# First nine input blocks all laid out with tokens on the partitions, and seven of them turned by VectorE

## What the reference computes

```python
u = rms_norm(h, norm_mix[l])
z = u @ w_in[l]
(aq, ak, av, bxin, bgate, cq, ck, cv, cf, dq, dk, dv, gz) = jnp.split(z, split_points, axis=-1)
ya = diff_attention(aq, ak, av, lam, slopes_a)                 # q, k: features x tokens
yb = rg_lru_branch(bxin, bgate, conv_w, conv_b, wa, ba, ...)   # scan along the tokens
yc = forgetting_attention(cq, ck, cv, logf)
yd = sliding_window_sink_attention(dq, dk, dv, sinks, slopes_d)
mixed = sum(gates[:, :, n] * (branches[n] @ w_branch[l, n]) for n in range(4))
```

## Time and profile before

| | |
|---|---|
| time, median of 3 runs (lowest, highest) | 2922.37 us (2922.26, 2922.62) |
| the profiled execution's own time | 2922.03 us |
| its span | 2920.2 us |
| TensorE busy | 2898.1 us, 99% |
| VectorE busy | 1906.7 us, 65% |
| ScalarE busy | 1363.7 us, 47% |
| granted TensorE clock, mean | 1.00 |

### The profile page before, as it was taken

One profiled execution on the slowest core, in us unless ns is written; L12 is line 12 of the kernel. 1 busy time (PEld: TensorE's weight loads), 2 busy tenths in 40 slices (PEclk: granted clock), 3 DMA queues, 4 the chain that ended last, 5 costly groups with the idle time before them and its releaser, 6 DMA issues.

```text
span 2920.2 us, 33076 instructions
## 1 busy us (share of the span) xinstructions
PE 2898.1 (99%) x13622; PEld 2420.9 (83%) x13622; DVE 1906.7 (65%) x2448; ACT 1363.7 (47%) x1755; POOL 61.9 (2%) x108
## 2 busy tenths in 40 slices
PE   8999999999999999999999999999999999999999
PEld 8998788888887888888888888888888888888887
DVE  5666675669877674577785544555897667457664
ACT  5545544444554443444446555444444444344443
POOL 1000000000011000000001000000000000000000
PEclk9999999999999999999999999999999999999999
DMA  7455555555566555555555445555555555555554
GB/s 267 158 185 183 178 184 180 199 202 189 204 245 221 200 193 196 189 200 188 190 200 195 160 172 184 171 178 194 192 199 195 194 190 199 188 197 191 189 200 159
DMA packets 84103, 561.76 MB, mean 192 GB/s; under 512 B 10067, under 2 KB 10211, under 8 KB 19056
## 3 DMA queue, kind: packets, MB, share of 16 engines
q1 hardware_dynamic: 77760, 544.80, 54.4%
q0 software_dynamic: 3456, 10.01, 1.2%
q10 hardware_dynamic: 2736, 4.83, 0.6%
HBM read 557.50 MB, written 3.68 MB: 192 GB/s over the span
## 4 chain that ended last, share of the span: by engine, by line
PE 98%; DVE 1%; ACT 0%; DMA 0%; issue 0%; DVEq 0%; ACTq 0%
PE acc L620 95%; PE misc L620 2%; PE misc L624 1%; DVE w_lo L1410 1%; DMA xT<-in_xT 0%; ACT w_hi L986 0%; DMA lam_vec<-in_lam_vectors 0%; ACT prob L965 0%; DVE lru_work L1662 0%; ACT u_hi L968 0%; DVE turned L1410 0%; DVE prob L1416 0%; ACT L965 0%; ACT av L968 0%; DVE y_lru_lo L1410 0%
## 5 line engine op out<-in xcount | busy, mean ns | idle before, releaser
L1410 DVE TENSOR_TENSOR w_lo<-raw,w_hi 128x1024 fp32r<-128x1024 f32 x1032 | 1256.5, 1220 | 837.4 <-ACT w_hi L986 830.9
L986 ACT ACTIVATE w_hi<-raw 128x1024 fp32r<-128x1024 f32 x1032 | 1087.4, 1056 | 1240.2 <-PE acc L620 1239.2
L620 PE MATMUL acc<-w_hi,v_hi 128*128 128x512 f32 x1408 | 548.1, 389 | 0.0
L620 PE MATMUL acc<-w_hi,v_lo 128*128 128x512 f32 x1408 | 547.8, 389 | 0.0
L620 PE MATMUL acc<-w_lo,v_hi 128*128 128x512 f32 x1408 | 547.7, 389 | 0.0
L620 PE MATMUL acc<-w_hi,u_hi 128*128 128x512 f32 (+1 forms) x1248 | 493.2, 395 | 0.0
L620 PE MATMUL acc<-w_hi,u_lo 128*128 128x512 f32 (+1 forms) x1248 | 483.3, 387 | 0.0
L620 PE MATMUL acc<-w_lo,u_hi 128*128 128x512 f32 (+1 forms) x1248 | 482.6, 387 | 0.0
L620 PEld LDWEIGHTS acc<-w_hi,v_hi 128*128 128x128 f32 x1408 | 264.3, 188 | 57.4 <-issue 2.6
L620 PEld LDWEIGHTS acc<-w_hi,v_lo 128*128 128x128 f32 x1408 | 264.3, 188 | 54.8
L620 PEld LDWEIGHTS acc<-w_lo,v_hi 128*128 128x128 f32 x1408 | 264.3, 188 | 54.7
(11 more groups left out here) (310 smaller groups left out, 2956.7 us busy)
## 6 DMA issues: line engine op xcount, KB each, us to landing
raw<-in_w_gates SPq DMA_DIRECT2D x112, 1024.0 KB, 4.9
raw<-in_w_ffn_gate SPq DMA_DIRECT2D x88, 1024.0 KB, 4.8
raw<-in_w_ffn_up SPq DMA_DIRECT2D x88, 1024.0 KB, 4.8
raw<-in_w_ffn_down SPq DMA_DIRECT2D x88, 1024.0 KB, 4.8
raw<-in_w_in SPq DMA_DIRECT2D x67, 1024.0 KB, 4.8
raw<-in_w_out SPq DMA_DIRECT2D x32, 1024.0 KB, 4.8
raw<-in_w_branch SPq DMA_DIRECT2D x24, 1024.0 KB, 4.8
raw<-in_w_mem SPq DMA_DIRECT2D x8, 1024.0 KB, 4.9
```

The source lines that it names most:

```text
L620: return e.matmul(o, w, x, start=start, stop=stop, skip_group_check=True)
L986: e.activation(m.w_hi[:, n % PART_SLOTS, 0:HALF_KT * cols], m.raw[:, c % RAW_SLOTS, o * cols:(o + HALF_KT) * cols], ACT.Copy).then_inc(s[" ...
L1410: return e.tensor_tensor(o, a, b, op)
```

## The change

All nine blocks are computed with tokens on the partitions. Their inverse roots are then a column, and ScalarE applies them when it evacuates the accumulator. For `keep4` and `keep8` it writes to the final place, as before. The other seven go to a staging buffer `keep_tok`, and a new mover `keep_turn` on VectorE turns them in 16 transposes of 32 x 256 elements, four in each of the first four steps of the next block. One staging buffer serves all seven. The constant factors of the queries are put into two more columns (`r_q64`, `r_q128`). The row of inverse roots with its diagonal matrices, two products and copy is gone. Those who read the seven results now wait on `keep_turned`.

The order of the tasks is the same; `rows` has two steps fewer.

```diff
-    plan = [full(f"keep{b}", "w_in", b, "u", fm=0 if b == 4 else 4) for b in range(5)]
+    plan = [full(f"keep{b}", "w_in", b, "u") for b in range(5)]
...
+KEEP_TURNED = (0, 1, 2, 3, 5, 6, 7)
...
         evacuate("keep", plan[f"keep{b}"], b)
+        if b in KEEP_TURNED:
+            mover(f"keep_turn:{b}", plan[f"keep{b}"], b)
...
# TensorE, stream: the products of one row tile
-                for f in range(b.fm):
-                    o = v[:, f // 2, (f % 2) * SEQ:(f % 2 + 1) * SEQ]
-                    mm = matmul(o, tile(whi, f), lhi, first and f % 2 == 0, last)
-                    mm = matmul(o, tile(whi, f), llo, False, last)
-                    mm = matmul(o, tile(wlo, f), lhi, False, last)
...
+                for t in range(2):
+                    o = v[:, t, 0:b.cols]
+                    mm = matmul(o, tile(lhi, t), whi, first, last)
+                    mm = matmul(o, tile(lhi, t), wlo, False, last)
+                    mm = matmul(o, tile(llo, t), whi, False, last)
...
# TensorE, rows
-        matmul(bank[:, 0:P], m.ones[:, 0:P], m.diag_r[:, 0, :], True)
-        matmul(bank[:, P:2 * P], m.ones[:, 0:P], m.diag_r[:, 1, :], False).then_inc(s["rows_summed"], 1)
...
# ScalarE, evacuate
+        if kind == "keep":
+            n = more[0]
+            to, scale = m.keep[n], {2: m.r_q64, 5: m.r_q64, 6: m.r_q128}.get(n, m.r_mix)
             e.wait_ge(s["half_read"], b.done)
             e.wait_ge(s["row_root"], 1)
+            if n in KEEP_TURNED:
+                to = m.keep_tok
+                if n:
+                    e.wait_ge(s["keep_turned"], KEEP_TURNED.index(n))
...
+            scaled(to[:, 0, :], v[:, 0, :], scale[:, 0:1])
+            scaled(to[:, 1, :], v[:, 1, :], scale[:, 1:2]).then_inc(freed, 1)
...
# ScalarE, rows
-        scaled(m.r_rows[:, :], bank[:, 0:SEQ], 1.0).then_inc(s["rows_copied"], 1)
...
# VectorE, evacuate
-        if kind == "keep" and b.fm:
-            ...
-            stt(to[:, 0:2, :], v[:, 0, :].rearrange("p (a b) -> p a b", a=2), scale, rows, ALU.mult, ALU.mult)
-            stt(to[:, 2:4, :], v[:, 1, :].rearrange("p (a b) -> p a b", a=2), scale, rows, ALU.mult,
-                ALU.mult).then_inc(freed, 1)
...
# VectorE, rows
-        for t in range(2):
-            i = ts(m.diag_r[:, t, :], m.ident[:, :], m.r_mix[:, t:t + 1], ALU.mult)
+        ts(m.r_q64, m.r_mix, 64 ** -0.5, ALU.mult)
+        ts(m.r_q128, m.r_mix, 128 ** -0.5, ALU.mult).then_inc(s["q_scales"], 1)
+
+    def keep_turn(block, b):
+        e.wait_ge(s[f"acc_freed{block.slot}"], block.after)
+        yield from turn_squares(m.keep_tok[:, :, :], m.keep[b], 4, "keep_turned")
...
+    def turn_squares(tokens, turned, steps, done):
         squares = tokens.rearrange("p t (m n b) -> p t m n b", m=4, n=4)
         to = turned[:, :, :].rearrange("p m (t i b) -> p t m i b", t=2, i=4)
         for n in range(16):
             i, f = divmod(n, 4)
             mm = e.transpose(to[32 * f:32 * f + 32, :, :, i, :], squares[32 * i:32 * i + 32, :, :, f, :])
             if n == 15:
+                mm.then_inc(s[done], 1)
+            if (n + 1) % (16 // steps) == 0:
                 yield
```

More of the change, by code:

```diff
@@ L35, with __init__ @@
 class Block:
-    def __init__(self, label, name, b, k0, kn, cols, left, fm=0, frees=1):
+    def __init__(self, label, name, b, k0, kn, cols, left, frees=1):
         self.label, self.name, self.b, self.k0, self.kn, self.cols = label, name, b, k0, kn, cols
-        self.left, self.fm, self.frees = left, fm, frees
+        self.left, self.frees = left, frees
 def stream_plan():
     full = lambda label, name, b, left, **kw: Block(label, name, b, 0, KT, BW, left, **kw)
-    plan = [full(f"keep{b}", "w_in", b, "u", fm=0 if b == 4 else 4) for b in range(5)]
+    plan = [full(f"keep{b}", "w_in", b, "u") for b in range(5)]
     plan += [Block("keep_misc", "w_in_misc", 0, 0, KT, P + 4 + P, "u")]
-    plan += [full(f"keep{b}", "w_in", b, "u", fm=0 if b == 8 else 4) for b in range(5, 9)]
+    plan += [full(f"keep{b}", "w_in", b, "u") for b in range(5, 9)]
     for n, y in enumerate(("y_lru", "y_diff", "y_win", "y_fox")):
@@ L365, in __init__ @@
         self.q_sums, self.k_sums = spot("q_sums", r, 0, [4, SEQ]), spot("k_sums", r, 4, [4, SEQ])
-        self.diag_r, self.r_rows = spot("diag_r", q, 0, [2, P]), spot("r_rows", q, 1, [SEQ])
+        self.keep_tok = spot("keep_tok", q, 0, [2, BW])
         self.gate_w, self.decay, self.drive = (spot("lru_gate_w", q, 4, [8, P]), spot("decay", q, 8, [4, SEQ]),
@@ L622, in transposes @@
     def transposes(o, tiles, done):
+        need(("ident_landed", 16))
         for i, a in enumerate(tiles):
@@ L676, in rows, with turned @@
     def rows():
[L677 to L680, removed]
-        matmul(bank[:, 0:P], m.ones[:, 0:P], m.diag_r[:, 0, :], True)
-        matmul(bank[:, P:2 * P], m.ones[:, 0:P], m.diag_r[:, 1, :], False).then_inc(s["rows_summed"], 1)
-        bank_free[i] = ("rows_copied", 1)
+        yield 7
+    def keep_turn(block, b):
+        yield 4
+    def turned(b):
+        return ("keep_turned", KEEP_TURNED.index(b) + 1)
     def lru():
@@ L724, in diff @@
             banks = [task_bank(), task_bank()]
-            need(freed(plan["keep2"]))
-            need(freed(plan["keep3"]))
+            need(turned(2))
+            need(turned(3))
             paired_scores([bank for _, bank in banks], m.aqT[:, h, :], m.akT[:, h, :], "diff_pe")
@@ L760, in win @@
             need(("win_dve", WIN_DVE("dk")))
-            need(freed(plan["keep5"]))
+            need(turned(5))
             paired_scores([bank for _, bank in banks], m.dqT[:, j, :], m.dkT, "win_pe")
@@ L792, in fox @@
             need(("consts_landed", 16 * 11))
-            need(freed(plan["keep6"]))
-            need(freed(plan["keep7"]))
+            need(turned(6))
+            need(turned(7))
             need(("fox_dve", FOX_DVE("terms")))
@@ L949, in dil @@
             yield
-    work = {"x_move": x_move, "rows": rows, "lru": lru, "diff": diff, "win": win, "fox": fox, "gate_tanh": gate_tanh,
+    work = {"x_move": x_move, "rows": rows, "keep_turn": keep_turn, "lru": lru, "diff": diff, "win": win, "fox": fox, "gate_tanh": gate_tanh,
             "mixed_move": mixed_move, "row_squares": row_squares, "resid_move": resid_move, "ffn_rows": ffn_rows,
@@ L992, in bias_in @@
         if q == 0:
-            e.wait_ge(s[f"acc_freed{plan['keep7'].slot}"], plan["keep7"].after)
+            e.wait_ge(s["keep_turned"], len(KEEP_TURNED))
         elif q == 1:
@@ L1015, in evacuate @@
         freed = s[f"acc_freed{b.slot}"]
-        if kind == "keep" and not b.fm:
+        if kind == "keep":
+            n = more[0]
+            to, scale = m.keep[n], {2: m.r_q64, 5: m.r_q64, 6: m.r_q128}.get(n, m.r_mix)
             e.wait_ge(s["half_read"], b.done)
             e.wait_ge(s["row_root"], 1)
-            scaled(m.keep[more[0]][:, 0, :], v[:, 0, :], m.r_mix[:, 0:1])
-            scaled(m.keep[more[0]][:, 1, :], v[:, 1, :], m.r_mix[:, 1:2]).then_inc(freed, 1)
+            if n in KEEP_TURNED:
+                to = m.keep_tok
+                if n:
+                    e.wait_ge(s["keep_turned"], KEEP_TURNED.index(n))
+            if n == 2:
+                e.wait_ge(s["q_scales"], 1)
+            scaled(to[:, 0, :], v[:, 0, :], scale[:, 0:1])
+            scaled(to[:, 1, :], v[:, 1, :], scale[:, 1:2]).then_inc(freed, 1)
         elif kind == "keep_misc":
@@ L1110, in rows, with keep_turn @@
                            "x_squares", 2 * j + t + 1)
-        yield 3
-        bank = task_bank()
-        e.wait_ge(s["rows_summed"], 1)
-        scaled(m.r_rows[:, :], bank[:, 0:SEQ], 1.0).then_inc(s["rows_copied"], 1)
+        yield 2
+    def keep_turn(block, b):
+        yield 4
     def lru():
@@ L1437, in evacuate @@
         freed = s[f"acc_freed{b.slot}"]
-        if kind == "keep" and b.fm:
[L1439 to L1444, removed]
-            stt(to[:, 0:2, :], v[:, 0, :].rearrange("p (a b) -> p a b", a=2), scale, rows, ALU.mult, ALU.mult)
-            stt(to[:, 2:4, :], v[:, 1, :].rearrange("p (a b) -> p a b", a=2), scale, rows, ALU.mult,
-                ALU.mult).then_inc(freed, 1)
-        elif kind == "biased_gate":
+        if kind == "biased_gate":
             q = more[0]
@@ L1511, in moved @@
             if n == 15:
-                mm.then_inc(s["moved_turned"], 1)
-            if (n + 1) % per_step == 0:
+                mm.then_inc(s[done], 1)
+            if (n + 1) % (16 // steps) == 0:
                 yield
+    def moved(left, j, tokens, turned, gain=None):
+        yield from turn_squares(tokens, turned, turn_steps(j, left), "moved_turned")
         turn["moved"] += 1
@@ L1608, in lru @@
         yield
-        e.wait_ge(s[f"acc_freed{plan['keep0'].slot}"], plan["keep0"].after)
+        e.wait_ge(s["keep_turned"], KEEP_TURNED.index(0) + 1)
         for f in range(4):
@@ L1644, in lru @@
         yield
-        e.wait_ge(s[f"acc_freed{plan['keep1'].slot}"], plan["keep1"].after)
```

(1 more changed line is left out.)

11 lines of the change are left out of this document (3 added, 8 removed).

## The result

| | before | after |
|---|---|---|
| time, median of 13 runs | 2922.68 us | 2928.54 us |
| lowest to highest | 2922.15 to 2924.26 | 2926.90 to 2930.13 |
| profiled execution, its span | 2922.03, 2920.2 | 2928.97, 2927.2 |
| TensorE matmuls | 13622 | 12946 |
| VectorE busy | 1906.7 us | 1946.0 us |

The ratio is 1.0019 with a 95% interval of 1.0011 to 1.0027: slower by 5.9 us between the medians, with 2931 forecast. The two profiled executions are 6.9 us apart, their spans 7.0.

What follows compares the result with a forecast made beforehand. TensorE, busy 99% of the span, was taken as the bound. Terms -8.6 - 0.45 + 0.4 + 7.3 + 7.6 + 2.4 = +8.65 us, added to the median 2922.4, gave about 2931 us; range 2924.5 to 2935.5.

Steps and rivals of the forecast that it cites:

- Matmuls of 512 columns: TensorE in the nine blocks: each block 1.25 us shorter, 1.1 in `keep0`; sum -8.6 us.
- Evacuations on ScalarE: Seven blocks' evacuations move from VectorE to ScalarE; this and waiting for the single `keep_tok` cost nothing.
- The wait at the gate product: TensorE waits for conv33, late because VectorE's steps hold transposes: +7.3 us.
- The wait of 0.4 us in `keep2`: TensorE waits for the last `w_lo` of `keep2`, behind three steps of 3.05 us and small columns: +0.4 us.
- The waits in `diff`: TensorE's waits from the first `prob` through `keep6`, `keep7` and `keep8`: sum +7.6 us.
- First `prob`: Its chain does not hang on TensorE's spacing, so what nine shorter halves give goes into the wait: +1.4 us.
- The clock: TensorE's clock falls after the wait of 7.3 us at the gate product: +2.4 us, bounds 0 and 2.4.
- B: Rival: the waits come but without the slow clock, 2928.6 us; chance 0.25.
- A: The forecast itself: 2931 us; chance 0.47.
- C: Rival: only the gate product's wait is real, `diff` has more room; 2922.4 us, with the clock 2925; chance 0.15.
- D: Rival: VectorE's time is hidden and the matmul spacing comes through; 2913 us, faster; chance 0.05.
- E: Rival: more waits, the tail of `lru` beside `keep_misc` also comes late; +3 us, 2934; chance 0.08.

Runs made afterwards that it cites:

- copies_only: Kernel after with one copy of 128x256 in place of four transposes in each of the four steps, so results are wrong; 2913.24 us.
- spread: Kernel after with two transposes in each of eight steps instead of four in each of four; 2924.79 us.
- two_spread: spread with two staging buffers instead of one; 2920.82 us.
- tasks_first_spread: Kernel after with two transposes in each of eight steps, and task pieces before mover pieces while a block is turned; 2926.70 us.
- two_tf_spread: tasks_first_spread with two staging buffers instead of one; 2917.40 us.
- double_turn: Kernel after with each of the 16 transposes done twice, the second into a buffer nobody reads; 2961.14 us (one run).
- tasks_first: Kernel after with each engine doing a step's task piece before its mover piece while a block is turned; 2919.59 us.
- filler: Kernel after with 26 matmuls of 512 columns on TensorE ahead of the first gate product, their result overwritten; 2926.05 us.

## Why the prediction was right, and where its sizes were off

**Matmuls of 512 columns: right.** 21.76 us a block, forecast 21.79. In copies_only, where none of the new waits is left, the span is 9.7 us shorter, forecast 9.05; 2.6 of the 9.7 lie in `keep0`, where 1.55 were forecast and the profiles scatter. The rule of the Trainium skill ("TensorE: Matmul & The Clock Gate", section "Wait — 56ns, not 53.3ns?"), by which the spacing would have given 1.6 us, does not agree with any of these traces.

**Evacuations on ScalarE: right in the kernel after, but only because the turning ended in time.** I had written that waiting for the single buffer costs nothing since the block before is turned in the first half of this one. With eight steps it cost 4 us (spread against two_spread) and 9 us (tasks_first_spread against two_tf_spread).

**The wait at the gate product: right in mechanism and size.** VectorE went on 7.1 us after the start of `keep2` (7.3 forecast), had no pause, and ended conv33 at S + 39.6 (40.4). TensorE came at S + 32.9 (33.1) and waited 6.9 us (7.3). copies_only, double_turn and tasks_first show that it is the transposes, and that their place counts.

**The wait of 0.4 us in `keep2`:** 0.1 us by the block's time.

**The waits in `diff`: right in kind, about 2 us too large in sum.** What a wait costs is more than its idle time, so I compare blocks with copies_only, where nothing is turned.

- First `prob`: +1.4 forecast, +0.2 measured (a wait of 1.76 us for 1.54). This term failed most. I took the chain to it as fixed at 28.7 us from the start of `keep5`. It took 27.6 (150.06 to 177.65), and as much in copies_only. Its pieces stand between weight halves that come earlier too; that this is the reason follows from the order and was not tried.
- `keep6`: 27.13 against 26.10 us, so 1.0 for the 1.2 forecast (copy and scaling).
- `keep7`: 25.45 against 24.18, so 1.3 for 1.5, with only 0.67 + 0.16 us idle.
- `keep8`: 28.00 against 24.05, so 3.95, of which the clock has 1 us or a little more. That leaves less than 3 for the 3.5 forecast; the wait on `prob` was 2.24, and the copy cost nothing.

**The clock: right that it falls, off in size and in number.** 1.7 us instead of 2.4 behind the gate wait (filler). And I had expected it once; it fell also behind 2.24 us in `keep8`, which took 0.4 us more than forecast although the wait was shorter. The two errors are of opposite sign, so that the clock's part of the sum is nearly right is luck. The Trainium skill's rule ("TensorE: Matmul & The Clock Gate", section "Part 1: The HAM clock gate"), that an idle engine falls back to the throttled state, agrees with both; no fall was seen behind the 2.9 us of two_tf_spread.

**Rivals.** B (waits, but no slow clock) is out by the granted clock of 0.50 and by filler, though its 2928.6 us is nearer to the median than A's 2931. That is luck: A's waits were about 2 us too large, and B leaves out about as much for the clock. C is out by the waits in `keep7` and `keep8`. D would have been 2913 us and is what copies_only measured. E is out: `keep4` and `keep_misc` together did not change.

**The sum.** +8.65 was forecast; it came to +7.0 between the spans and +5.9 between the medians. The waits in `diff` and at the gate product were too large together, and the second fall of the clock, which was not forecast, made up for part of it.

The kernel after scatters over 3.2 us and the one before over 2.1. In the profiles `keep0` took from 23.3 to 25.4 us in kernels whose first block is the same, so much of the scatter may lie in the first 40 us. Why was not tried.

## What to carry to other kernels

Average utilisation does not say whether added work is hidden: VectorE was 65% busy, and the same transposes cost 15 us, or about 1 (8.3 gained against 9.5 in copies_only), by where they stood in its order ahead of a result that TensorE fetches in a given step. Before moving work to an engine in strict order, write down its order from the last forced pause to each result that another engine fetches, and put what is fetched first and what is not behind. When work in such an order ends later, ask who waits for its buffer: here a single staging buffer turned a gain of 5 us into a loss.

## What the runs showed of the hardware that I had not expected

- TensorE's clock fell behind idle times of 6.9, 6.1, 5.2, 4.8, 3.8 and 2.2 us at the gate products and in `keep8`, and also behind 1.9 us (first `prob` in two_spread and two_tf_spread) and 1.8 us (`w_lo` in double_turn). It did not behind 2.9 us in two_tf_spread and 2.0 us in double_turn (granted 1.00 in both), nor behind the first `prob` of the kernel after (1.8 us). The length of the idle time alone does not decide it; what else does was not tried. The granted clock in the slow stretch of the kernel after was 0.50, and its four gate products took 2.04 us instead of 1.03.
- At the start of the kernel the spacing is that of 1.2 GHz while the granted clock is written as 1.00; in the middle of the program the record follows (0.50). In the first microseconds only the spacing tells.
